# Prompt attention weighs V with normalised, split probabilities in one fp32r product, output transposed

## The reference, cut to what matters

```python
def _fox_block(q_blk, cq_blk, qpos, k, v, ckT, kpos):
    s = jnp.einsum('bqhd,bkhd->bhqk', q_blk, k, preferred_element_type=jnp.float32) * (FOX_HD ** -0.5)
    s = s + (jnp.swapaxes(cq_blk, 1, 2)[..., :, None] - ckT[..., None, :])
    s = jnp.where(kpos[None, :] <= qpos[:, None], s, -jnp.inf)
    p = jax.nn.softmax(s, axis=-1)
    return jnp.einsum('bhqk,bkhd->bqhd', p.astype(v.dtype), v)
```

## Time and profile before

| what | value |
|---|---|
| median of 3 runs | 1702.13 us |
| span of the profiled execution | 1703.1 us |
| TensorE busy | 1601.3 us, 94% |
| VectorE busy | 819.5 us, 48% |
| ScalarE busy | 663.1 us, 39% |
| GpSimd busy | 236.0 us, 14% |
| passes of `stage_fox` | about 484 to 735 us of the span |

### The profile page before, as it was taken

The page is one execution under the profiler, slowest core; times in us unless marked ns, Lnnn a source line. Parts: engine busy times, 40 slices in busy tenths (PEclk is TensorE's granted clock), DMA queues, the critical chain, the costliest instruction groups (busy, mean ns, idle before and its releaser), DMA issues. The chain is left out here.

```text
span 1703.1 us, 25703 instructions
## 1 busy us (share of the span) xinstructions
PE 1601.3 (94%) x9847; PEld 1464.5 (86%) x9847; DVE 819.5 (48%) x1362; ACT 663.1 (39%) x1117; POOL 236.0 (14%) x292
## 2 busy tenths in 40 slices
PE   7999999999999999999999999999998599999980
PEld 7988898889989898999999999999787488888760
DVE  3433463353033433313032323233647799999975
ACT  5422241222254554522112111112212488888866
POOL 1000120013011111130000000000000254443220
PEclk9999999999999999999999999999998699999995
DMA  6111231125211112062325124111432899999736
GB/s 183 40 38 38 73 112 49 36 66 167 78 48 41 68 44 79 19 188 79 126 62 179 46 66 143 38 38 67 162 132 81 278 265 273 326 300 290 190 60 230
DMA packets 154225, 204.34 MB, mean 120 GB/s; under 512 B 14723, under 2 KB 121235, under 8 KB 154104
## 3 DMA queue, kind: packets, MB, share of 16 engines
q1 hardware_dynamic: 135224, 140.82, 26.3%
q0 software_dynamic: 18880, 61.89, 13.1%
HBM read 152.34 MB, written 50.34 MB: 119 GB/s over the span
## 5 line engine op out<-in xcount | busy, mean ns | idle before, releaser
L380 PE MATMUL ps<-xh,slab_hi 128*128 128x384 f32 (+1 forms) x504 | 171.8, 341 | 1.4 <-DVE slab_lo L732 1.4
L380 PE MATMUL ps<-xh,slab_lo 128*128 128x384 f32 (+1 forms) x504 | 165.1, 328 | 0.0
L380 PE MATMUL ps<-xl,slab_hi 128*128 128x384 f32 (+1 forms) x504 | 165.0, 327 | 0.0
L1899 PE MATMUL ps<-xh,slab_lo 128*128 128x384 f32 (+1 forms) x384 | 125.2, 326 | 0.0
L1899 PE MATMUL ps<-xh,slab_hi 128*128 128x384 f32 (+1 forms) x384 | 125.1, 326 | 0.0
L1899 PE MATMUL ps<-xl,slab_hi 128*128 128x384 f32 (+1 forms) x384 | 125.1, 326 | 0.0
L2100 DVE TENSOR_TENSOR gt_sg<-ps,gt_sg 128x384 f32<-128x384 f32 (+1 forms) x48 | 25.7, 536 | 186.5 <-PE ps L1899 186.3
L380 PEld LDWEIGHTS ps<-xh,slab_hi 128*128 128x128 f32 x504 | 95.0, 188 | 15.4 <-issue 13.6
L2869 PE MATMUL ps<-mo_hi_gu,mo_xh 128*128 128x512 f32 x256 | 100.3, 397 | 0.9 <-ACT mo_xh L2972 0.7
L2869 PE MATMUL ps<-mo_hi_gu,mo_xl 128*128 128x512 f32 x256 | 98.9, 391 | 0.0
L2040 ACT ACTIVATE gt_sg<-ps 128x384 f32<-128x384 f32 (+1 forms) x48 | 22.7, 473 | 191.1 <-PE ps L1899 191.1
(11 more groups left out here) (500 smaller groups left out, 4219.3 us busy)
## 6 DMA issues: line engine op xcount, KB each, us to landing
slab_raw<-in_w_in SPq DMA_DIRECT2D x60, 512.0 KB, 4.2
mo_raw_g<-in_w_e_gate SPq DMA_DIRECT2D x16, 1024.0 KB
mo_raw_u<-in_w_e_up SPq DMA_DIRECT2D x16, 1024.0 KB
mo_raw_d<-in_w_e_down SPq DMA_DIRECT2D x16, 1024.0 KB
gt_oh<-oT_hi SPq DMA_DIRECT2D x3, 2176.0 KB, 7.8
gt_ol<-oT_lo SPq DMA_DIRECT2D x3, 2176.0 KB, 12.7
slab_raw<-in_w_branch SPq DMA_DIRECT2D x24, 256.0 KB, 4.6
x_dram<-slab_raw SPq DMA_DIRECT2D x9, 512.0 KB, 5.1
```

The costliest lines, as they stand in the source:

```text
L380: mm = eng.matmul(out, w[:, b, k, :], x[:, k, t0:t0 + tn], start=(k == 0 and j == 0), stop=(k == KC - 1 and j == 2), skip_group_check=True)
L1899: last = eng.matmul(out, w[:, s % 2, c, wk, :], x[:, k, t0:t0 + tn], start=(k == 0 and i == 0), stop=(k == ks[-1] and i == 2))
```

## The change

The probabilities are normalised before they are transposed, on GpSimd (`normalise`: P times the reciprocal, in place), after both heads' exponentials and a reciprocal on VectorE (`row_inverse`, last in VectorE's pass). The transposed probabilities are split into a head (ScalarE's copy out of the bank, as fp32r) and a tail (VectorE's `probs_low`, bank minus head). A bank is free once the tail is made (`bank_freed`). V of a head pair is split once per pair into `vhl`, 64 columns of head beside 64 of tail (`split_values`). One product per key tile and head then has [V head | V tail] stationary and [P head | P tail] moving (256 columns). Its result is already transposed: three of its four quarters are added (ScalarE's `bring_low_half`, two additions in VectorE's `sum_parts`), then split by `out_head` and `out_tail`, now in 64 partitions with one buffer each. `transpose_out` goes. SyncE issues the stores of the output, the loads of `cb` (`rows`, one buffer per head) between its weight blocks, and the gate weights at passes 20 and 22; at its end it waits for all these stores. GpSimd keeps the stores of keys and values. In `stage_gates` GpSimd waits for the last output tail ahead of one memset, since `oT` lies in the same memory. `mpos` and `ident16` move to other memory.

```diff
-        P, PT = sb("P", [128, 3, SEQ]), sb("PT", [128, 2, 8, 128])
-        cb = sb("cb", [128, 4, SEQ])
-        o_tm = sb("o_tm", [128, 2, 2, HD])
-        oh, ol = sb("oh", [128, 2, 128], F32R), sb("ol", [128, 2, 128], F32R)
+        P, PT = sb("P", [128, 3, SEQ]), sb("PT", [128, 2, 8, 2, 128], F32R)
+        cb = sb("cb", [128, 2, SEQ])
...
+        vhl = sb("vhl", [128, 8, 2, 2, HD], F32R)
+        oh, ol = sb("oh", [HD, 2, 128], F32R), sb("ol", [HD, 2, 128], F32R)
...
+        def bank_freed(eng, C):
+
+            if C >= 2:
+                if C - 2 in prob_of:
+                    eng.wait_ge(pt_lo, BASE + prob_of[C - 2] + 1)
+                else:
+                    eng.wait_ge(pt_out, C - 1)
+
+        def rows(eng, p):
+            for h in range(2):
+                if p >= 1:
+                    eng.wait_ge(s_out, last(out_no, 8 * p - 1, h) + 1)
+                eng.dma_start(cb[:, h, :],
+                              sh.c_dram[0, 2 * p + h:2 * p + h + 1, 0:SEQ].broadcast_to([128, SEQ])).then_inc(c_in[h], 16)
...
+            def normalise(Q):
+                kn = 128 * (Q % 8 + 1)
+                eng.wait_ge(rinv_done, Q + 1)
                 for h in range(2):
-                    eng.dma_start(cb[:, 2 * (p % 2) + h, :],
-                                  sh.c_dram[0, 2 * p + h:2 * p + h + 1, 0:SEQ].broadcast_to([128, SEQ])).then_inc(c_in[p % 2], 16)
+                    I = 2 * Q + h
+                    eng.tensor_scalar(P[:, I % 3, 0:kn], P[:, I % 3, 0:kn], rinv[:, Q % 2, h:h + 1], None,
+                                      ALU.mult).then_inc(pool_s, 1)
...
             store_keys(0)
+            normalise(0)
+            for Q in range(NQ):
+                if Q < 24 and Q % 8 == 4:
+                    store_keys(Q // 8 + 1)
+                if Q + 1 < NQ:
+                    normalise(Q + 1)
+            eng.wait_ge(v_st, 32)
+            eng.wait_ge(k_st, 32 * 4)
...
+            for n in range(RW, 9):
+                load_block(n)
+                if n == 5:
+                    eng.wait_ge(pool_s, 4)
+                    rows(eng, 0)
             for Q in range(NQ):
                 p, qt = divmod(Q, 8)
+                if p < 3 and qt == 5:
+                    rows(eng, p + 1)
                 eng.wait_ge(oT_lo, Q + 1)
-                store_branch(sh, eng, 1, slice(128 * p, 128 * p + 128), slice(128 * qt, 128 * qt + 128),
-                             oh[:, Q % 2, :], ol[:, Q % 2, :], o_st[Q % 2])
-                if p < 3 and qt == 4:
-                    store_keys(p + 1)
-                if p < 2 and qt == 7:
-                    rows(p + 2)
+                for dst, src in ((sh.oT_hi, oh), (sh.oT_lo, ol)):
+                    eng.dma_start(dst[1, 128 * p:128 * p + 128, 128 * qt:128 * qt + 128].rearrange("(h d) n -> d h n", h=2),
+                                  f32(src[:, :, :])).then_inc(o_st[Q % 2], 16)
+                if Q in (0, 4, 8):
+                    load_block(9 + Q // 4)
+                if Q == 20:
+                    eng.wait_ge(pages_in, 16)
+                    eng.wait_ge(w_tail, NBLK)
+                    eng.wait_ge(p_tr, k_chunk[3, 2] + 1)
+                    load_gates(sh, eng, 0)
+                if Q == 22:
+                    load_gates(sh, eng, 1)
             for i in range(2):
                 eng.wait_ge(o_st[i], 32 * (NQ // 2))
...
             def transpose_probs(Q, h):
                 I = 2 * Q + h
-                eng.wait_ge(exp_done, I + 1)
+                eng.wait_ge(pool_s, 4 + I + 1)
                 for c in range(n_chunk(Q)):
                     C = chunk_no[Q, h, c]
-                    if C >= 2:
-                        eng.wait_ge(pt_out, C - 1)
+                    bank_freed(eng, C)
                     for t in range(4 * c, min(4 * c + 4, Q % 8 + 1)):
                         mm = eng.transpose(sh.ps[:, 5 + C % 2, 128 * (t % 4):128 * (t % 4) + 128],
                                            P[:, I % 3, 128 * t:128 * t + 128], sh.ident[:, :])
                     mm.then_inc(p_tr, 1)
 
-            def transpose_out(Q):
-                eng.wait_ge(o_out, Q + 1)
-                eng.transpose(sh.ps[:, 7, 128:256], o_tm[:, Q % 2, :, :].rearrange("p h d -> p (h d)"),
-                              sh.ident[:, :]).then_inc(oT_tr, 1)
-
             def weigh_values(Q, h):
                 p, qt = divmod(Q, 8)
                 if h == 0 and Q >= 1:
-                    eng.wait_ge(oT_lo, Q)
-                eng.wait_ge(pt_out, last(chunk_no, Q, h) + 1)
+                    eng.wait_ge(oT_sum, BASE + 2 * Q)
+                if h == 0 and qt == 0:
+                    eng.wait_ge(v_tail, p + 1)
+                eng.wait_ge(pt_lo, BASE + last(out_no, Q, h) + 1)
                 for t in range(qt + 1):
-                    mm = eng.matmul(sh.ps[:, 7, 64 * h:64 * h + 64], PT[:, h, t, :],
-                                    v[:, t, 64 * (2 * p + h):64 * (2 * p + h) + 64],
+                    mm = eng.matmul(sh.ps[:, 7, 256 * h:256 * h + 256], vhl[:, t, h, :, :].rearrange("p s d -> p (s d)"),
+                                    PT[:, h, t, :, :].rearrange("p s n -> p (s n)"),
                                     start=(h == 0 and t == 0), stop=(t == qt), skip_group_check=True)
                 mm.then_inc(pv_done, 1)
...
                 transpose_probs(Q, 0)
-                if Q >= 1:
-                    transpose_out(Q - 1)
                 piece(Q, 1)
                 transpose_probs(Q, 1)
...
-                    eng.activation(PT[:, h, 4 * c:4 * c + nt, :].rearrange("p t n -> p (t n)"),
-                                   sh.ps[:, 5 + C % 2, 0:128 * nt], ACT.Copy).then_inc(pt_out, 1)
+                    eng.activation(PT[:, h, 4 * c:4 * c + nt, 0, :],
+                                   sh.ps[:, 5 + C % 2, 0:128 * nt].rearrange("p (t n) -> p t n", t=nt),
+                                   ACT.Copy).then_inc(pt_out, 1)
+
+            def split_values(p):
+                if p == 0:
+                    eng.wait_ge(pool_s, 4)
+                    eng.wait_ge(*sh.front.state_st)
+                else:
+                    eng.wait_ge(pv_done, 16 * p)
+                eng.activation(vhl[:, :, :, 0, :], v[:, :, 128 * p:128 * p + 128].rearrange("p t (h d) -> p t h d", h=2),
+                               ACT.Copy).then_inc(v_head, 1)
+
+            def bring_low_half(Q):
+                eng.wait_ge(pv_done, 2 * Q + 2)
+                if Q >= 1:
+                    eng.wait_ge(oT_lo, Q)
+                eng.activation(oT[:, :, :], sh.ps[HD:128, 7, :].rearrange("p (h s n) -> p h s n", h=2, s=2)[:, :, 0, :],
+                               ACT.Copy).then_inc(oT_low_half, 1)
 
             def out_head(Q):
-                eng.wait_ge(oT_tr, Q + 1)
-                if Q >= 2:
-                    eng.wait_ge(o_st[Q % 2], 32 * (Q // 2))
-                eng.activation(oh[:, Q % 2, :], sh.ps[:, 7, 128:256], ACT.Copy).then_inc(oT_hi, 1)
+                eng.wait_ge(oT_sum, BASE + 2 * Q + 2)
+                if Q >= 1:
+                    eng.wait_ge(o_st[(Q - 1) % 2], 32 * ((Q - 1) // 2 + 1))
+                eng.activation(oh[:, :, :], oT[:, :, :], ACT.Copy).then_inc(oT_hi, 1)
...
             exponent(0, 1)
             for Q in range(NQ):
+                if Q >= 1:
+                    bring_low_half(Q - 1)
+                if Q % 8 == 0:
+                    split_values(Q // 8)
                 place_unit(Q, 0)
                 place_probs(Q, 0)
                 if Q + 1 < NQ:
                     exponent(Q + 1, 0)
-                if Q >= 1:
-                    out_head(Q - 1)
                 place_unit(Q, 1)
                 place_probs(Q, 1)
                 if Q < 24 and 2 <= Q % 8 <= 4:
                     store_key_tiles(Q // 8 + 1, Q % 8 - 2)
+                if Q >= 1:
+                    out_head(Q - 1)
...
-            def normalise(Q):
-                ch(eng.reciprocal(rinv[:, Q % 2, :], rsum[:, Q % 4, :]))
-                eng.wait_ge(pv_done, 2 * Q + 2)
+            def row_inverse(Q):
+                eng.wait_ge(exp_done, 2 * Q + 2)
                 if Q >= 2:
-                    eng.wait_ge(oT_tr, Q - 1)
-                eng.tensor_tensor(o_tm[:, Q % 2, :, :], sh.ps[:, 7, 0:128].rearrange("p (h d) -> p h d", h=2),
-                                  rinv[:, Q % 2, :].unsqueeze(2).broadcast_to([128, 2, HD]), ALU.mult).then_inc(o_out, 1)
+                    eng.wait_ge(pool_s, 4 + 2 * (Q - 1))
+                eng.reciprocal(rinv[:, Q % 2, :], rsum[:, Q % 4, :]).then_inc(rinv_done, 1)
+
+            def split_values(p):
+                eng.wait_ge(v_head, p + 1)
+                eng.tensor_tensor(vhl[:, :, :, 1, :], v[:, :, 128 * p:128 * p + 128].rearrange("p t (h d) -> p t h d", h=2),
+                                  f32(vhl[:, :, :, 0, :]), ALU.subtract).then_inc(v_tail, 1)
+
+            def probs_low(Q, h):
+                for c in range(n_chunk(Q)):
+                    C = chunk_no[Q, h, c]
```

(58 more changed lines are left out.)

36 lines of the change are left out of this document (18 added, 18 removed).

## The result

The changed kernel took 1734.07 us (median of 4 runs, 1733.17 to 1741.97) against 1702.09 for the kernel before on the same chip: ratio 1.0194, 95% interval 1.0179 to 1.0209. The forecast was 1706 us with a range of 1688 to 1719: the sign is right, the size is not. A second measurement gave 1731.04 us, ratio 1.0173 (1.0158 to 1.0189). The profiled execution has a span of 1733.0 us, 29.9 more than before.

The account below looks back on a forecast made before the run. TensorE's queue was taken as the bound. A to D cost 38.4 us against 40.2 removed, minus 1.8; with the clock losses of E the sum was plus 5, shaded to plus 4: 1706 us, range 1688 to 1719.

Parts of the forecast that it names:

- Removed: TensorE work removed, minus 40.2 us: 34.4 from single-pass value products, 3.5 and 0.4 from output transposes, 1.9 from unit-copy waits.
- A: In passes over 512 keys, the second head's transposes wait for VectorE's subtraction behind `lowest`: plus 20.7 us, 16 to 25.
- B: Narrower passes: key transposes at position 3, waits at positions 2 and 0: plus 4.8 us, bounds 1 and 8.
- C: Transposes wait for both heads' exponentials, VectorE's reciprocal and GpSimd's multiply, priced at 1.1 us: plus 8.7 us.
- Rival 3: GpSimd's multiply takes 2 us or more, binding passes over 768 keys too: plus 7, 1713 us; chance 0.09.
- D: Both ends: first pass waits 1.2 us, first key page at the handover 3.0 (1.5 to 6): plus 4.2 us.
- E: Half clock after TensorE's new waits, losses of 1.7 us each: plus 6.8 us; 0 to 20 us held possible.
- two sure and two more: Half-clock losses: after the wait of pass 22 and at the end, and two among the 12 wide passes.
- Rival 2: The lower clock follows most wide passes, 8 to 10 losses of 1.7 us: 1718 us; chance 0.12.
- the shading: The forecast's sum of plus 5 us lowered to plus 4, as some relief was surely missed.
- Rival 1: Added waits are not additive, as ScalarE and VectorE catch up: minus 15, 1687 us; chance 0.26.
- Rival 4: The value product steps at two passes as before and gains nothing: 1740 us; chance 0.01.

Follow-up runs that it names:

- run 9: Each value product issued twice into its bank, against the kernel with head-by-head VectorE multiply, earlier subtraction and earlier page loads: 1725.45 us, ratio 1.0131.
- Run 3: VectorE's subtraction of (Q, 0) put ahead of the unit tail and the minimum of (Q+1, 1), against the changed kernel: 1724.24 us, ratio 1.0135.
- run 1: Scaling of the probabilities left out (no GpSimd multiply, no reciprocals), against the changed kernel: 1711.69 us, ratio 1.0049.
- run 6: Multiply moved from GpSimd to VectorE, both heads behind the reciprocal at the same queue place, against the changed kernel: 1730.01 us, ratio 1.0176.
- run 10: Key transposes behind the third piece, query tail ahead in pass 21, against the kernel with head-by-head VectorE multiply, earlier subtraction and earlier page loads: 1693.58 us.
- run 7: Reciprocal and multiply on VectorE, head by head and ahead of the last unit tail and weight tails, against the changed kernel: 1714.06 us, ratio 1.0076.
- run 5: Last pass's stores put behind the second page load, against the changed kernel, measured twice: 1730.55 us (ratio 1.0161) and 1731.2 us (ratio 1.0176).
- 8: Head-by-head VectorE multiply, subtraction ahead of the minimum and page loads ahead of the last stores, all in the changed kernel: 1699.39 us, ratio 0.9989.

## Why the prediction was wrong

By its own steps, each against the ledger of the profiled execution:

- **Removed: minus 40.2, measured minus 32.** The product steps went from 66.0 to 41.0 us, minus 25.0 and not 34.4. Their step is 0.119, so 288 of them are 34.3; but I subtracted from 67.8 us of record time, where the steps sum to 66.0 (0.112 from one old product to the next, not 0.118), left out the 2.7 us of the last step of each pass (before the scores), and the rest is waits for the second head's subtraction and a little half clock. That one product is one pass the 288 records at this step show, and run 9 again. The output transposes brought 4.2 (forecast 3.9). Waits for unit copies brought 0.8 (1.9), and 1.9 more went that the sum did not have, at two unit tails and at the gate copies. Before:

```profile
PE ps L1200 <- DVE slab_lo L1479: 1.5, 2, 1.1
PE ps L1609 <- ACT m L1373: 1.2, 3, 0.5
```

- **A and B: plus 25.5, measured plus 19.6** (15.6 for P, 6.2 - 2.2 for keys). A was right place by place; start to start, position 4 lost 1.22 us (forecast 1.2), position 5 2.07 (2.15), position 6 1.50 (1.5). Run 3 shows the cause, the order in VectorE's queue. Of B the key transposes at position 3 came as priced (3 x 0.6, forecast 3 x 0.55); positions 0 and 2 show no such wait, so 3.1 of its 4.8 us were not there.
- **C: plus 8.7, measured plus 22 to 23** (trace, run 1). This is the step that failed. Its structure was right in the main: passes 2, 10, 18 and 27 waited 1.2 to 1.3 us each (forecast 1.0), and 23 longest (5.0 for 2.75); the term was mis-sized through the multiply, 2.85 us for 1.1. The bounds failed as well: I had bounded a read-and-write on GpSimd from a memset, by an argument (reading costs as much again) that no row carried. Rival 3 named this case and its threshold of 1.6 us, but priced it at plus 7 where it was plus 13, since it moved only passes over 768 keys; at 2.5 ns a column passes 4, 12 and 20 with 640 keys waited 0.6 each (priced at 0.25), and 6 and 14 waited 1.55 (0.6). The sum had nothing at position 7, where the second head also waits for its own multiply behind the first one: 6.4 us in passes 7, 15 and 31, 0.8 to 1.8 at each head. The Trainium skill's GPSIMD Engine Reference, section 4.1, sends elementwise work to VectorE; 755 against 2846 ns for the same instruction agrees. What the Trainium skill says there of one-input operations, roughly at line rate on GpSimd, does not hold for this one, 3.8 times as long as on VectorE. The estimate of 1.5 us from section 3.1 of that page of the Trainium skill would have been too low here by almost a half.
- **D: plus 4.2, measured plus 9.8 and 5.8** in two profiles. The first pass cost nothing. The page wait was 5.5 and 3.8 us (forecast 3.0, bounds 1.5 and 6), with stores that landed later than priced (3.45 and 2.7 us for 1.8), and half clock behind it made the rest.
- **E: plus 6.8, then shaded by 1.** In the stage it was 6.4 us against 1.0 before (half of the time that TensorE's steps took in the stretches, idle time left out); 0.6 of it is in the product steps above, and the handover's is in D. The forecast of "two sure and two more" stretches was close: four new ones. Rival 2 (most wide passes) did not come; run 6 came nearest to it, with 11.7 us.
- **Not in the sum: about plus 2.4.** The idle time that the profile shows before an instruction is less than what a wait costs:

```profile
596.66 0.34 PE L1236 MATMUL ps<-xh,slab_lo 128*128 128x384 f32 x1
598.91 0.52 PE L1294 MATMUL ps<-ident,fx_P 128*128 128x128 f32 x3 [1.91 <-DVE fx_PT L1569]
```

Without a wait the transpose starts 0.17 us after that piece, at 596.83. It starts at 598.91, 2.08 later, with 1.91 shown. Over the 44 waits of the stage some 53 us were lost and 46.6 shown, 0.14 a wait; the 17 waits of the stage before hid 3.9 us in the same way, so 2.4 are new.

The measured terms: - 25.0 - 4.2 - 2.7 + 19.6 + 22.1 + 9.8 + 4.8 + 2.4 = 26.8, against 29.9; the ledger does not place the last 3 us. Of the 26 us between the forecast's 4 and the 29.9, C's price is 13.4, the products' 9.4, D's 5.6, the hidden part of waits 2.4, what is not placed 3.1 and the shading 1.0, less 5.9 for A and B, 2.0 for E and 1.1 for the other relief. So C is the largest miss, and the products' gain the second: with C priced at 22.1 and all else as it was, the sum gives 1719.4 us, at the edge of the range. Rival 1 (waits not additive) is refuted for this kernel in its main claim, that waits vanish behind one another: 46.6 us of them stand in the stage. But taking one part away did not give all of it back as fewer waits: run 1 took 22.1 us of them and 6 came back, run 3 took 12.7 and 5 came back. Rival 4 fell with the 288 records at 0.119 us.

## What to carry to other kernels

Price an operation on an engine from a row of that operation on that engine; where there is none, its bound must be wide enough to reach the next rival, and it is worth asking early whether another engine could do it. When work is added to a chain between engines, its place in each queue can cost as much as its length: moving the multiply to VectorE, a quarter as long, gained 1 us at the old place behind the weight tails, and 18 us in front of them and head by head. A change that frees TensorE time and adds waits can be worth having once the orders are put right: here 1.8% slower became 0.5% faster with the same products, and only in the second round of orders (run 10).

## What the runs showed of the hardware

- GpSimd's multiply by a per-row scalar, fp32 in SBUF, takes 0.29 us and 2.5 ns a column at 128 partitions; VectorE's takes 0.76 us at 1024 columns (run 7).
- A fp32r product with 128x128 stationary and 256 moving columns steps at 0.119 us; issued twice in a row with the same stationary operand it steps at 0.120, no faster (run 9). The fp32 product with 64 moving columns took two records of 0.112 each.
- The granted clock fell to 0.50 (1.2 GHz) at each wait of 3.7 us or more, at the handover and at pass 23. After shorter waits it fell in some cases and not in others. In run 6 it fell at a wait of 2.9 us at 686 us and not at one of 2.9 at 544. At the handover it fell with a wait of 1.7 us (run 5, first profile) and of 2.4 (run 9), and not with one of 1.7 in run 5's second profile. At the start of the stage the same wait of 1.67 us stands in all 14 profiles, the kernel before included, and the clock fell within 2.2 us of its end in 7 of them. At position 4, after waits of 1.05 to 1.25 and 1.46 us in close order, it fell at one or two of the three pairs of a profile, and where the first of the pair was 2.0 us or more (run 6) at all three. With the first one down to 0.4 us it fell at none in runs 3 and 8 and at one in run 9; with the key transposes moved behind the third piece at none. Once (821 us) it fell with no wait ahead, among products of 16 and 64 moving columns. What decides in these cases stays open, and one profile of a kernel does not tell how often it falls.
